# A mixture-of-experts layer: expert outputs scaled at the eviction and added to the residual by scattered, accumulating DMA, instead of stored and gathered at the end

## What is computed

```python
h2 = rms_norm(x, moe_norm_w)
top_v, top_i = lax.top_k(h2 @ router_w + router_b, 4)      # 4 of 32 experts for each token
gates = jax.nn.softmax(top_v)
gu = xb @ w_gu[e] + b_gu[e]                                # xb: the rows of h2 that chose expert e
act = (up + 1.0) * (gate * sigmoid(1.702 * gate))          # gate and up: clamped halves of gu
y = act @ w_down[e] + b_down[e]
x = x + sum over the token's 4 experts of gates * y
```

## Time and profile before

| | |
|---|---|
| median of three executions | 2752.41 us (2729.75 to 2755.03) |
| the profiled execution | 2754.21 us |
| its span, first to last instruction | 2752.4 us |
| TensorE clock granted, mean over the span | 0.881 of full speed |
| busy share: PE, DVE, ACT, POOL | 87%, 58%, 45%, 14% |
| stage 6, first gather to last eviction | 1052.0 to 2663.4 us |
| stage 7 | 2682.0 to 2752.4 us |

### The profile page before, as it was taken

How to read it: one execution, slowest core, us unless ns; L and a number is a source line. 1 busy time by engine, 2 the same in 40 slices (tenths; PEclk the granted TensorE clock), 3 DMA queues, 4 the chain that set the end, 5 groups by cost and what they waited for, 6 DMA issues and landing times. The chain is left out here.

```text
span 2752.4 us, 37463 instructions
## 1 busy us (share of the span) xinstructions
PE 2381.7 (87%) x12171; PEld 1996.3 (73%) x12172; DVE 1591.2 (58%) x1855; ACT 1242.6 (45%) x1613; POOL 395.9 (14%) x456
## 2 busy tenths in 40 slices
PE   4899947799996915999999999999999999999960
PEld 3788745577775815878788878888777788787850
DVE  4421066443332154666876677676788866876655
ACT  4112132222222113565665666565666656666540
POOL 1420025011000042010110010010011100101004
PEclk7999978755567957999999999999999999999985
DMA  3123130600003245687997799697899977998759
GB/s 132 71 81 108 50 77 21 227 1 1 0 1 132 107 119 171 220 281 257 330 323 235 236 297 303 224 308 236 265 355 345 349 255 247 343 307 288 246 184 365
DMA packets 421755, 556.92 MB, mean 202 GB/s; under 512 B 29060, under 2 KB 308613, under 8 KB 421701
## 3 DMA queue, kind: packets, MB, share of 16 engines
q1 hardware_dynamic: 408677, 513.46, 56.5%
q0 software_dynamic: 13024, 42.75, 4.3%
HBM read 500.67 MB, written 55.49 MB: 202 GB/s over the span
## 5 line engine op out<-in xcount | busy, mean ns | idle before, releaser
L1403 DVE TENSOR_TENSOR VL<-RAW,VH 128x2048 fp32r<-128x2048 f32 x389 | 887.8, 2290 | 322.5 <-ACT VH L1398 280.3
L1398 ACT ACTIVATE VH<-RAW 128x2048 fp32r<-128x2048 f32 x390 | 725.9, 1908 | 54.0 <-DMA RAW<-in_expert_w_gate_up 47.5
L1763 PE MATMUL banks<-T,VH 128*128 128x384 f32 x1920 | 549.0, 360 | 3.9 <-issue 2.2
L1765 PE MATMUL banks<-T,VL 128*128 128x192 f32 x1680 | 422.1, 251 | 0.0
L1763 PEld LDWEIGHTS banks<-T,VH 128*128 128x128 f32 x1920 | 354.8, 189 | 5.4 <-issue 4.5
L1765 PEld LDWEIGHTS banks<-T,VL 128*128 128x128 f32 x1680 | 322.6, 192 | 0.6
L164 PE MATMUL banks<-VH,A 128*128 128x512 f32 (+1 forms) x752 | 302.0, 402 | 0.0
L166 PE MATMUL banks<-VH,A 128*128 128x512 f32 (+1 forms) x752 | 300.8, 400 | 0.0
L165 PE MATMUL banks<-VL,A 128*128 128x512 f32 (+1 forms) x752 | 300.0, 399 | 0.0
L166 PE MATMUL banks<-VH,T 128*128 128x512 f32 x544 | 212.4, 390 | 0.0
L165 PE MATMUL banks<-VL,T 128*128 128x512 f32 x544 | 212.2, 390 | 0.0
(11 more groups left out here) (295 smaller groups left out, 3385.8 us busy)
## 6 DMA issues: line engine op xcount, KB each, us to landing
RAW<-in_expert_w_gate_up SPq DMA_DIRECT2D x264, 1024.0 KB
RAW<-in_expert_w_down SPq DMA_DIRECT2D x130, 1024.0 KB
dY<-yb SPq DMA_DIRECT2D x98, 128.0 KB
RAW<-in_w_in SPq DMA_DIRECT2D x6, 2048.0 KB, 8.9
dY<-zeros SPq DMA_DIRECT2D x17, 512.0 KB, 10.8
dY<-yb SPq DMA_DIRECT2D x32, 256.0 KB
xin<-in_x SPq DMA_DIRECT2D x8, 512.0 KB
RAW<-in_w_out SPq DMA_DIRECT2D x2, 2048.0 KB
```

Source lines behind the costliest of these rows:

```text
L1398: act.activation(VH[:, i, ks], RAW[:, i, ks], ACT.Copy).then_inc(s_hi, 1)
L1403: dve.tensor_tensor(VL[:, i, ks], RAW[:, i, ks], VH[:, i, ks].bitcast(f32), ALU.subtract).then_inc(s_w, 1)
L1763: last = pe.matmul(o[:, 0:2 * NW].rearrange("p (a n) -> p a n", a=2), VH[:, c % 3, k, col], T2[:, :, k], start=k == 0, stop=k == KT - 1)
L1765: pe.matmul(o[:, 0:NW], VL[:, c % 3, k, col], T2[:, 0, k], start=False, stop=False)
```

## The change

Stage 7 is gone, and `dY` with it. `dX1` is now two tensors in HBM, one for each half of the columns, each with 256 spare rows behind the 1024 real ones. In stage 5 the gates are computed before `pos`, and the scatter into `dTok` carries pairs (token, gate); `dTok` is pre-filled with spare rows and gate 0, so that an empty slot points to a spare row of its own. A second table `gall` holds the gate of each slot. The number of superblocks and which are wide stays as it was; units are counted as 2 for a narrow and 3 for a wide superblock.

In stage 6, ACT multiplies with the gate at the eviction (`scale=gcur`). **POOL** then adds the rows to `dX1` with an indirect DMA that accumulates (`compute_op=ALU.add`): two a narrow superblock, with 128 rows of 2 KB each, and four a wide one (128 and 64 rows for each half). In a narrow superblock a DMA of 128 single floats (`dPad`) follows each, so that the counts of the semaphores stay equal. Since two superblocks may hold the same token, POOL waits at the start of each for the scatters of the one before (`s_st`), **ahead of** the gather. At the end SP waits for the last scatters and copies both halves from HBM to HBM into the output. The memset of `yb` moves from DVE to POOL.

```diff
-SBMAX = S * TOPK // UN + NE
-SLOTS = (SBMAX + 2) * UN
+SBMAX = S * TOPK // UN + 2 * NE
+SLOTS = (SBMAX + 4) * UN
+SPARE = 4 * UN
...
-                for b in range(S * TOPK // P, SLOTS // P):
-                    sp.dma_start(dY[b * P:(b + 1) * P, :].rearrange("p (a c) -> p a c", a=2), bc(zeros[:].unsqueeze(1), [P, 2, CH])).then_inc(s_filled, 16)
+                for b in range(SPARE // P):
+                    rows = slice(S + b * P, S + (b + 1) * P)
+                    for i in range(2):
+                        sp.dma_start(dX1[i][rows, :], zeros[:]).then_inc(s_filled, 16)
+                        sp.dma_start(dH2[rows, i * CH:(i + 1) * CH], zeros[:]).then_inc(s_filled, 16)
...
-                                            tokid[:, i // TOPK:i // TOPK + 1], None).then_inc(s_sc, 16)
+                                            slot[:, i // TOPK, i % TOPK], None).then_inc(s_sc, 16)
...
+                dve.wait_ge(s_e, 1)
+                link(dve.tensor_reduce(gsum[:], g4[:], X, ALU.add))
+                link(dve.reciprocal(gsum[:], gsum[:]))
+                dve.tensor_tensor(slot[:, :, :, 1], g4[:], bc(gsum[:].unsqueeze(2), [P, TT, TOPK]), ALU.mult).then_inc(s_pos, 1)
                 dve.tensor_copy(pos[:], posf[:]).then_inc(s_pos, 1)
...
-                dve.tensor_copy(idxall[:, 0:SBMAX], ps[2][:, 0:SBMAX]).then_inc(s_ix, 1)
+                dve.tensor_copy(idxall[:, 0:SBMAX], ps[2][:, 0:SBMAX])
+                dve.tensor_copy(gall[:, 0:SBMAX], ps[2][:, SBMAX:2 * SBMAX]).then_inc(s_ix, 1)
...
                         load(sp, (c + 5) % NCH, e if c == 0 else en)
-                        if c >= GU:
-                            wait(s_ea, s * N2 + (2 * c + 6))
-                            for q in range(2):
-                                at = (c - GU) * CH + q * HC
-                                sp.dma_start(dY[bass.ds(fb * UN, P), at:at + HC], yb[:, c % 2, q * HC:(q + 1) * HC]).then_inc(s_st[c % 2], 16)
...
+                for i in range(2):
+                    wait(s_st[i], n * 32 + 16)
+                for i in range(2):
+                    sp.dma_start(out2[:, i * CH:(i + 1) * CH], dX1[i][0:S, :]).then_inc(s_out, 16)
...
+                def begin(s):
+                    f0 = pool.value_load(tab[0:1, bass.ds(s, 1), 1:2], min_val=0, max_val=SBMAX - 1)
+                    f1 = pool.value_load(tab[0:1, bass.ds(s + 1, 1), 1:2], min_val=0, max_val=SBMAX - 1)
                     en = pool.value_load(tab[0:1, bass.ds(s + 1, 1), 0:1], min_val=0, max_val=NE - 1)
+                    for i in range(2):
+                        wait(s_st[i], s * 32 + 16)
+                    pool.tensor_copy(scur[:], idxall[:, bass.ds(f0, 3)]).then_inc(s_cur, 1)
+                    pool.tensor_copy(gcur[:], gall[:, bass.ds(f0, 3)]).then_inc(s_cur, 1)
...
+                def narrow(s):
+                    en = begin(s)
+                    for i in range(2):
+                        wait(s_ea, s * N2 + (2 * (GU + i) + 6))
+                        pool.indirect_dma_start(dX1[i], bass.IndirectOffsetOnAxis(ap=scur[:, 0:1], axis=0), yb[:, i], None, compute_op=ALU.add).then_inc(s_st[i], 16)
+                        pool.dma_start(dPad[i], onec[:]).then_inc(s_st[i], 16)
+                        if i == 0:
+                            next_biases(s, en)
...
+                pool.memset(yb[:], 0.0).then_inc(s_y0, 1)
+                pool.wait_ge(s_y0, 1)
+                for i in range(2):
+                    pool.dma_start(dX1[i][S:S + P, :], yb[:, i]).then_inc(s_st[i], 16)
                 pool.tensor_copy(icur[:], idxall[:, 0:3]).then_inc(s_ic, 1)
...
-                            act.activation(yb[:, c % 2], ps[2 * (c % 2)], ACT.Copy).then_inc(s_ea, 2)
+                            act.wait_ge(s_cur, s * 2 + 2)
+                            act.activation(yb[:, c % 2], ps[2 * (c % 2)], ACT.Copy, scale=gcur[:, 0:1]).then_inc(s_ea, 2)
...
-    for stage_ in (stage1, stage2, stage3, stage4, stage5, stage6, stage7):
+    for stage_ in (stage1, stage2, stage3, stage4, stage5, stage6):
         run(stage_)
```

More of the change, by code:

```diff
@@ L131, in layer_kernel @@
     dQK = dram("dQK", [4 * P, S])
-    dX1, dH2 = dram("dX1", [S, D]), dram("dH2", [S, D])
-    dTok = dram("dTok", [SLOTS, 1])
-    dY = dram("dY", [SLOTS, D])
+    dX1 = [dram(f"dX1{i}", [S + SPARE, CH]) for i in range(2)]
+    dH2 = dram("dH2", [S + SPARE, D])
+    dTok = dram("dTok", [SLOTS, 2])
+    dPad = [dram(f"dPad{i}", [P, 1]) for i in range(2)]
     dTab = dram("dTab", [SSB + 1, 3], i32)
@@ L1016, in layer_kernel @@
     rowkey = ext.take("rowkey", [P, 2])
+    gall = ext.take("gall", [P, SBMAX + 3])
     E1 = ext.at
@@ L1149, in layer_kernel @@
     posf = r5.take("posf", [P, TT * TOPK])
+    pos = r5.take("pos", [P, TT * TOPK], u32)
     rank = r5.take("rank", [P, TT, NE])
@@ L1307, in _ @@
                     dve.tensor_copy(btT[:, :, 6 * q:6 * q + n], ps[4 + q][:, 0:2 * n * NE].rearrange("p (g i e) -> p g i e", g=2, i=n))
[L1309 to L1312, removed]
                 dve.memset(idxall[:, SBMAX:SBMAX + 3], 0)
+                dve.memset(gall[:, SBMAX:SBMAX + 3], 0.0)
                 for c in range(3):
@@ L1362, in layer_kernel @@
     icur = r6e.take("icur", [P, 3], u32)
+    scur = r6e.take("scur", [P, 3], u32)
+    gcur = r6e.take("gcur", [P, 3])
     btT = r6e.take("btT", [P, 2, 2 * GU, NE])
@@ L1481, in _ @@
                     load(sp, c + 3, e0)
-                n = superblocks(sp, narrow, wide)
+                n = superblocks(sp, body, body)
+                for i in range(2):
+                    wait(s_st[i], n * 32 + 16)
+                for i in range(2):
+                    sp.dma_start(out2[:, i * CH:(i + 1) * CH], dX1[i][0:S, :]).then_inc(s_out, 16)
                 for i in range(3):
                     wait(s_raw[i], n * 64 + (64 if i < 2 else 32))
-                for i in range(2):
-                    wait(s_st[i], n * 32 + 16)
+                sp.wait_ge(s_out, 32)
             @block.gpsimd
@@ L1515, in body, with next_biases @@
                     wait(s_ic, s + 2)
                     gather()
+                    wait(s_cur, s * 2 + 2)
+                    return en
+                def next_biases(s, en):
                     wait(s_bu, s + 1)
                     biases(bass.ds(s + 1, 1), en, s + 2)
+                def narrow(s):
+                    en = begin(s)
+                    for i in range(2):
+                        wait(s_ea, s * N2 + (2 * (GU + i) + 6))
[3 more added lines that the diff above has]
+                            next_biases(s, en)
@@ new lines, in wide @@
+                def wide(s):
+                    en = begin(s)
+                    for i in range(2):
+                        for h in range(2):
+                            m = height(h)
+                            wait(s_ea, s * N2 + (2 * (GU + i) + h + 5))
+                            pool.indirect_dma_start(dX1[i], bass.IndirectOffsetOnAxis(ap=scur[0:m, 2 * h:2 * h + 1], axis=0), yb[0:m, h], None, compute_op=ALU.add).then_inc(s_st[h], 16)
+                        if i == 0:
+                            next_biases(s, en)
@@ L1524, in _ @@
                 biases(slice(0, 1), e0, 1)
-                n = superblocks(pool, body, body)
+                n = superblocks(pool, narrow, wide)
+                for i in range(2):
+                    wait(s_st[i], n * 32 + 16)
                 wait(s_xg[0], n * 16 + 16)
@@ L1674, in wide @@
                         first_half(s, c)
-                dve.memset(yb[:], 0.0).then_inc(s_y0, 1)
                 dve.sem_inc(s_a, 2)
```

109 lines of the change are left out of this document (31 added, 78 removed).

## The result

The changed kernel takes 2815.91 us in the median of four executions (2811.9 to 2818.58); the one before, run beside it, 2753.72. The ratio is 1.0244, with a 95% interval of 1.0185 to 1.0303: slower by some 62 us, where 2712 us and a gain were forecast. The profiled execution has a span of 2810.2 us, 57.8 more than before.

The account below looks back on a forecast made before the run. Wide superblocks were held bound by PE, narrow by PE and DMA almost equally. 2752.4 - 63.5 (end) + 3.7 (start) + 0.5 (stage 5) + 17 (narrow) = 2710.1; with 1.8 beyond the span, 2712 us, range 2688 to 2752.

Parts of the forecast that it names:

- (a): Narrow superblocks: reading back the rows added to costs DMA time, 0.7 us each (0 to 3).
- (c): Narrow superblocks: POOL's wait for earlier scatters delays the gather, but 4.4 us are in hand, so it costs nothing.
- (b): Narrow superblocks: scatter and pad ahead of hot_e on POOL make it late for PE, 0.3 us each (0 to 2).
- The scatter lands too late: Rival, chance 0.11: POOL's wait delays the gather; from landing time L = 14.3 us slower than before, at 18 2817 us.
- The end: End of the kernel: stage 7 goes, a copy to the output follows SP's last load; 63.5 us saved.
- a slow copy: Rival at the end, chance 0.07: the copy runs at a quarter of the rate, 40 us instead of 12, total 2740.
- The start of stage 6: POOL's memset and two DMAs ahead of the first gather count in full: 3.7 us (2 to 6).
- The second read: Narrow superblocks: each accumulating scatter reads back 0.52 MB in all, 1.46 us a superblock at 359 GB/s.
- Wide superblocks: 15 superblocks: PE is full and the read fits into the free fifth of DMA; cost zero.

Follow-up runs that it names:

- e5: The changed kernel with the pad's 128 writes of 4 bytes each 2 KB from the next instead of side by side: 2707.06 us.
- e3: The changed kernel, pad kept, with POOL's gather of the next tokens issued ahead of its wait for the scatters: 2807.68 us.
- e2: The kernel before plus only the pad, in every superblock, its semaphore not waited for before the end of the stage: 2921.04 us.
- e10: e9 with POOL's memset of yb and two DMAs of zeros moved behind the first gather and first biases: 2701.03 us, ratio to before 0.9786.
- e7: The changed kernel with the pad written as one row of 512 bytes from one partition: 2661.15 us.
- e9: The changed kernel with the pad as one row of 512 bytes and hot_e made ahead of the scatters: 2700.73 us, ratio to before 0.9843.
- e11: e1 with the narrow superblocks' scatters plain instead of accumulating, so part of the sum is missing: 2722.25 us.
- e4: The changed kernel, pad and waits kept, with the narrow superblocks' scatters plain instead of accumulating, so part of the sum is missing: 2774.37 us.
- e12: The changed kernel with the pad's 128 writes of 4 bytes each 64 bytes from the next instead of side by side: 2707.06 us.
- e1: The changed kernel without the pad, each narrow scatter of 128 rows issued as two of 64: 2726.44 us, ratio to before 0.99.

## Why the prediction was wrong

*The step that failed* is (a) of the narrow superblocks, the term "DMA work", for which 0.7 us was taken with bounds of 0 and 3. It counted what the scatter reads back and gave the pad nothing, without a reason. The pad was even named, in (c), where it got "landed 7.4 later" from the gathers. It lands in 17.5 us, and for that time the engines move half of what they did (186 GB/s at a share of 1.04). The rows of before held no transfer of that shape in stage 6, and I did not set its bounds apart from the scatter's. Besides, (a) up to 3 and (b) up to 2 were added to "0 to 3" without a reason. Measured, it is 10.9 us for each of the ten narrow superblocks behind a narrow one, nearly all by the pad (e5: 1.0 us with the writes apart), 1.4 for each of the seven wide ones behind a narrow one, and nothing for the seven narrow ones behind a wide one, whose stretch holds no pad.

*Where it decides.* "the next wide superblock clears a backlog, but in a row of narrow ones it builds up" was right in kind. With the earlier trace rows's share of 1.08 a narrow superblock has no DMA time to give, with 0.80 a wide one has: the wide stretch above takes two pads with its share going from 0.83 to 1.02 and lasts 0.2 us longer.

*The rival that came out at the right number was the wrong one.* "The scatter lands too late" gave 2817 us at L = 18; the measured L is 17.5 and the time 2816. But its mechanism, tokens that reach PE late, is worth 6 us (e3), and the pad costs as much in a kernel where POOL waits for no scatter (e2). That 17 times 6.2 us and ten times 10.9 come out alike is chance. One DMA was behind both, the wait on POOL and the late weights, and the chain of waits told them apart before any experiment: PE waited for `qa` and ACT for `RAW`, not PE for `xg`.

*The end*: forecast 63.5 us, measured 60.7. The start of the copy came out to a tenth of a microsecond behind SP's last load; the copy from HBM to HBM took 14.2 us from issue to landing for 4.19 MB, and with the rest of the end 18.0 instead of 15.1. The rival of a slow copy fell.

*The start of stage 6*: forecast 3.7, measured 4.2 (13.19 against 9.03 us of waiting for the first gather). e10 suggests that the sum was right for a partly wrong reason: only 1.5 us come back when POOL's work is moved away, and the gather itself takes longer (8.2 us from issue to PE's start in the changed kernel, 6.4 before).

*(b), `hot_e`*: forecast 0.3 us a narrow superblock, 5 in all; PE's waits for it are 6.8 us in the changed kernel, and from e7 to e9, where only it is moved, stage 6 shrinks by 2.1. The rule of the Trainium skill that the prediction draws on (SBUF — State Buffer, "Who interferes with whom"), about VectorE instructions with two inputs in SBUF, was borne out again: in the changed kernel the same scatter of 128 rows takes 3.55 us on POOL beside DVE's pair of splits (at 2130.05) and 1.66 when it starts while none of them runs (at 2138.22).

*The second read*: forecast up to 1.46 us a superblock, 25 in all; 5.5 us over stage 6 without the pad (e11), 30 with it (e4). The Trainium skill (Collectives: The Full Stack, "The bandwidth ceiling: the fold count and why AG ≠ RS ≠ AR") puts the price of a sum down to its second read. Without the pad this kernel stays under the 25 us that the forecast worked out for the bytes of such a read; with it, it does not. The profile shows the read only in part: with plain scatters there are 2176 packets less, 64 for each narrow scatter, but the bytes it counts are the same 529.31 MB.

*Wide superblocks*: forecast zero, measured +0.6 us in all for the six behind a wide one and +9.5 for the seven that have pads under way; 5.0 of these stand in a single one.

Had the pad been harmless, the forecast would have stood. e5 and e12 change nothing but the pad's target: stage 6 is 12.4 and 13.8 us longer than before, where 17 were forecast, and the time is 2707.06 us, where 2712 was. With `hot_e` moved as well, stage 6 in e9 is 3.9 us longer than before, the end 60.7 shorter, the start 4.4 longer, together 52 us of gain, and the median fell from 2751.39 to 2700.73.

## What to carry to other kernels

- A DMA that only pads a semaphore's count is a DMA. Write it as one row, or leave 64 bytes between its elements; two pads of 128 floats side by side from 128 partitions cost this kernel eleven microseconds wherever the DMA engines had no room, and about one where they had.
- Where DMA share is near 1, watch GB/s beside it: an unchanged share with fewer GB/s says that something small fills the engines, and the waits of the largest stream (here ACT for `RAW`) say who pays.
- Storing scaled rows by accumulating scatter instead of storing, gathering and adding at the end pays here, 2751 to 2701 us. What PE needs next from POOL should stand ahead of the scatters: that was worth 24 us with two scatters of 64 rows each, and 2, no more than two traces differ by, with one of 128, where PE then waited for the gather instead. A wait that is gone from the list is not yet time saved.

## What the runs showed of the hardware

- 128 writes of 4 bytes at 4 bytes' distance: 17.5 us to landing in the median (14.5 to 20.8), and 186 GB/s for all DMA meanwhile. At 64 bytes' distance 6.9 us, at 2 KB 7.0 us and 350 GB/s. One row of 512 bytes 6.8 us, 128 rows of 2 KB 7.5 us. Each is a median beside full weight traffic, from one execution; the GB/s are those of one window each. The Trainium skill (DMA: Bandwidth & Descriptors, "Specifications") says that transfers under 512 bytes are a read, change and write back; by that alone the writes apart should be dear too, and here they are not. The measurement decides: small size cost little, single floats of 128 partitions with neighbours much. Distances between 4 and 64 bytes were not tried, nor was it shown what in the memory makes such writes wait.
- The accumulating scatters (64 or 128 rows of 2 KB) land in 6.3 us in the median beside full weight traffic, in the changed kernel as in e1; in e11, which is e1 with those of the narrow superblocks plain, the median of all is 5.8.
- A copy of 4.19 MB from HBM to HBM in two DMAs, with nothing beside it: 14.2 us from issue to landing.
